# Moving four full-precision products of the last block ahead of its second layer, and weighing and adding half by half

## The reference, cut to what matters

```python
def expert_block(args):
    xblk, e = args
    return (jax.nn.silu(xblk @ w1[e]) * (xblk @ w3[e])) @ w2[e]

yb = lax.map(expert_block, (xb.reshape(n_blocks, MOE_BLOCK, D), block_e)).reshape(-1, D)
y = (yb[dest] * wts.reshape(-1)[order][:, None]).astype(xf.dtype)
return jnp.zeros_like(xf).at[tok].add(y)
...
x = x + gx2 * _moe(hx.reshape(-1, D), ...).reshape(x.shape)
return _rmsnorm(x, norm_f)
```

## Time and profile before

| | |
|---|---|
| median of 3 runs | 892.17 us (891.77 to 892.59) |
| the profiled execution's own time | 892.63 us |
| its span | 890.9 us |
| busy in the span: TensorE, VectorE, ScalarE, GpSimd | 858.4, 635.9, 415.1, 194.5 us |
| chain that ended last: TensorE, VectorE, DMA | 78%, 11%, 5% |

### The profile page before, as it was taken

How to read it: one execution, slowest core, us unless ns; L and a number is a source line. 1 busy time by engine, 2 the same in 40 slices (tenths; PEclk the granted TensorE clock), 3 DMA queues, 4 the chain that set the end, 5 groups by cost and what they waited for, 6 DMA issues and landing times.

```text
span 890.9 us, 14102 instructions
## 1 busy us (share of the span) xinstructions
PE 858.4 (96%) x4980; PEld 706.8 (79%) x4981; DVE 635.9 (71%) x907; ACT 415.1 (47%) x597; POOL 194.5 (22%) x225
## 2 busy tenths in 40 slices
PE   8999999999999999999879999999999999999993
PEld 6789878888997567887678888888888888888872
DVE  1678755789777748556875769399936648599995
ACT  3485456201224441232253457378634525487772
POOL 4042001100000101111033323233313222234324
PEclk9999999999999999999969999999999999999997
DMA  9953566511035032222799759979997596699984
GB/s 342 344 179 110 171 194 211 152 43 57 8 142 191 1 142 81 109 79 102 261 338 329 245 170 370 303 245 379 377 361 255 174 307 220 176 342 379 370 331 177
DMA packets 82359, 195.31 MB, mean 219 GB/s; under 512 B 4919, under 2 KB 13324, under 8 KB 82314
## 3 DMA queue, kind: packets, MB, share of 16 engines
q1 hardware_dynamic: 71168, 158.87, 49.6%
q0 software_dynamic: 8272, 25.84, 11.2%
q10 hardware_dynamic: 2874, 10.01, 2.8%
HBM read 169.57 MB, written 25.71 MB: 219 GB/s over the span
## 4 chain that ended last, share of the span: by engine, by line
PE 78%; DVE 11%; DMA 5%; issue 2%; ACT 2%; POOL 1%; ACTq 0%; SPq 0%; POOLq 0%; DVEq 0%
PE ps L2455 16%; PE ps L2443 12%; PE ps L2104 9%; PE ps L2460 8%; PE ps L2107 7%; PE ps L2437 2%; PE ps L2304 2%; DMA raw<-in_w_dram 2%; PE ps L2295 1%; DVE arena L1420 1%; PE ps L2297 1%; PE ps L2296 1%; DMA raw<-x_rows 1%; PE ps L2246 1%; PE ps L2160 1%
## 5 line engine op out<-in xcount | busy, mean ns | idle before, releaser
L1144 ACT ACTIVATE wah<-raw 128x2048 fp32r (+1 forms) x32 | 61.4, 1919 | 65.6 <-issue 32.8
L1853 DVE TENSOR_TENSOR wbl<-raw,wbh 128x2048 fp32r<-128x2048 f32 x32 | 73.1, 2288 | 5.2 <-ACT wbh L1144 4.5
L2443 PE MATMUL ps<-w2h,hTh 128*128 128x512 f32 x184 | 76.1, 413 | 0.5 <-DVE hTl L1863 0.5
L2455 PE MATMUL ps<-wbh,xTh 128*128 128x512 f32 x184 | 73.9, 402 | 0.0
L2455 PE MATMUL ps<-wah,xTh 128*128 128x512 f32 x184 | 72.3, 393 | 0.0
L775 POOL DMA_INDIRECT x_rows<-late_rows,block_dst x21 | 49.9, 2375 | 102.8 <-DVE late_rows L1868 102.8
L2443 PE MATMUL ps<-w2h,hTl 128*128 128x512 f32 x184 | 72.3, 393 | 0.0
L2443 PE MATMUL ps<-w2l,hTh 128*128 128x512 f32 x184 | 72.1, 392 | 0.0
L2455 PE MATMUL ps<-wal,xTh 128*128 128x512 f32 x184 | 72.1, 392 | 0.0
L1853 DVE TENSOR_TENSOR wal<-raw,wah 128x2048 fp32r<-128x2048 f32 x30 | 68.8, 2292 | 4.5 <-issue 3.2
L1853 DVE TENSOR_TENSOR w2l<-raw,w2h 128x2048 fp32r<-128x2048 f32 x32 | 71.8, 2282 | 0.0
(11 more groups left out here) (412 smaller groups left out, 2178.0 us busy)
## 6 DMA issues: line engine op xcount, KB each, us to landing
raw<-in_w_dram SPq DMA_DIRECT2D x64, 1024.0 KB
raw<-in_w_dram SPq DMA_DIRECT2D x16, 2048.0 KB
arena<-in_w_mod_dram SPq DMA_DIRECT2D x32, 512.0 KB, 4.1
arena<-in_x_dram SPq DMA_DIRECT2D x16, 512.0 KB, 9.7
arena<-in_w_mod_dram SPq DMA_DIRECT2D x3, 2048.0 KB, 13.7
arena<-in_w_in_dram SPq DMA_DIRECT2D x6, 1024.0 KB, 6.8
x_rows<-arena ACTq DMA_DIRECT2D x9, 512.0 KB, 3.1
hx_rows<-arena ACTq DMA_DIRECT2D x9, 512.0 KB, 4.4
```

The costliest lines, as they stand in the source:

```text
L1144: act.activation(high_half, raw_half, ACT.Copy).then_inc(w_high[j], 1)
L1853: dve.tensor_tensor(low_half, raw_half, high_half.bitcast(F32), ALU.subtract).then_inc(w_split[j], 1)
L2443: ins = pe.matmul(out_ap, parts[l][:, lhs], w_parts[w][:, cols], start=start and n == 0, stop=stop and n == 2)
L2455: pe.matmul(ps[:, 2 + j, :], xTh[:, k * P:(k + 1) * P], w[:, k * HALF:(k + 1) * HALF], start=(k == 0 and w is wh), stop=False)
```

## The change

The four full-precision products move from behind the last block's second layer to ahead of it, behind the first layer and ahead of the wait for the first half of `hTh` and `hTl`. They count on another semaphore (`rank_done` in place of `l2_done`), and they bring their waits with them. On VectorE the loop over weighing and the loop over adding become one, so that each half is weighed and then added; two increments of a counter go.

```diff
@@ VectorE, end of the last block
             for h in range(2):
                 dve.wait_ge(S["l2_done" if h else "l2_half"], last + 1)
                 weigh_half(last, h, last_y)
-            for h in range(2):
                 cols = slice(h * HALF, (h + 1) * HALF)
                 dve.wait_ge(S["y_ready"], 2 * last + (h + 3))
-                dve.wait_ge(S["l2_done"], last + (h + 2))
-                dve.sem_inc(S["load_seen"], 1)
+                dve.wait_ge(S["rank_done"], h + 5)
                 dve.tensor_tensor(last_x[:, cols], ps[:, h, :], last_y[:, cols], ALU.add).then_inc(S["last_sum"], 1)
@@ TensorE, expert(), after the first layer
                 if more:
                     turn_block(b + 1)
+                else:
+                    pe.wait_ge(S["slots_done"], 5)
+                    pe.wait_ge(S["gathered"], 16 * b + 48)
+                    pe.wait_ge(S["y_ready"], y_count)
+                    for h in range(2):
+                        cols = slice(h * HALF, (h + 1) * HALF)
+                        pe.matmul(ps[:, h, :], ident[:, :], last_x[:, cols], start=True, stop=False)
+                        pe.matmul(ps[:, h, :], same_tok, ysb[:, 0, cols], start=False, stop=True).then_inc(S["rank_done"], 1)
                 pe.wait_ge(S["hT_a"], b + 1)
                 pe.wait_ge(S["y_ready"], y_count)
@@ TensorE, after the last block
             expert(last, NE - 1, 2 * last + 2, False)
-            pe.wait_ge(S["slots_done"], 5)
-            pe.wait_ge(S["gathered"], 16 * last + 48)
-            for h in range(2):
-                cols = slice(h * HALF, (h + 1) * HALF)
-                pe.matmul(ps[:, h, :], ident[:, :], last_x[:, cols], start=True, stop=False)
-                pe.matmul(ps[:, h, :], same_tok, ysb[:, 0, cols], start=False, stop=True).then_inc(S["l2_done"], 1)
```

## The result

| | median | runs |
|---|---|---|
| before, 12 runs | 892.07 us | 890.80 to 892.59 |
| changed, 12 runs | 894.01 us | 892.38 to 894.26 |

The changed kernel is slower: the ratio is 1.0021, with a 95% interval of 1.0013 to 1.0028, that is 1.2 to 2.5 us. The forecast was 894.0.

A forecast was written before the change was run, and what follows sets the result against it. The last block was taken as bound by ScalarE, GpSimd's roots and VectorE, with TensorE's end products hidden. Terms 1.82 + 0.03 = 1.85 us on 892.17 gave 894.0 us; own range with run scatter 893.3 to 894.8, with rivals 892.3 to 895.4.

The forecast's parts named there:

- Steps 1 and 2: TensorE: products leaving the end (3.44 us) were hidden, worth nothing; at the new place they start at 865.92 without waiting.
- Step 3: TensorE behind the products: second layer starts 3.12 us later, shrinking to 2.11 us at the second hidden half's transposes.
- Step 4: ScalarE's copy of the second hidden half starts 0.42 us after the transposes, 1.82 us later than before.
- Step 5: Behind the copy: ScalarE's squares with GpSimd's roots, and VectorE's low part with its finishes, both move by 1.82 us.
- Step 6: VectorE weighing and adding half by half: 2.84 us in place of 2.60, net cost 0.03 us.
- step 7: Queue operations: two increments dropped on VectorE, nothing (-0.05 to 0); three more TensorE waits, nothing (0 to 0.1).
- Rival A: GpSimd's roots slip by one VectorE finish, 1.19 us more, about 895.2 us; chance 0.12 together with D.
- B: Rival: the delay on the way from ScalarE's copy to the weighing is absorbed, no change, 892.2 to 893.5; chance 0.15.
- C: Rival: VectorE's adds were waiting for TensorE's products, so moving them saves up to 1.5 us, 890.7; chance 0.07.
- D: Rival: a late gather holds the products at their new place, 1 us later giving 895.0; chance 0.12 together with Rival A.

The follow-up runs named there:

- e3: The changed kernel with the four products placed behind the transposes of the second hidden half: 891.91 us against 891.92 us for the kernel before.
- e5: The changed kernel with only half 0's two products ahead of the second layer, half 1's two left at the end: 892.21 us, ratio 1.0005 to the kernel before.
- e7: The changed kernel with ScalarE squaring row tile 7 ahead of its copy of the second hidden half: 893.11 us, ratio 1.0011 to the kernel before.
- e2: The kernel before with only VectorE's order changed to half by half, products left at the end: 892.38 us, ratio 1.0003.
- e1: The changed kernel with VectorE's old order (weigh, weigh, add, add), so only the products moved: 893.94 us against 891.92 us for the kernel before.
- e9: e2 with the end products counting on rank_done, so VectorE waits for constants and the counter increments are gone: ratio 1.0001 to the kernel before.
- e4: Against the kernel before: one product in TensorE's wait, half 0 weighed and added between finishes, early rows last, the two indirect stores swapped: ratio 0.9998.
- e8: Against the kernel before: tile 3's gain and ScalarE's second-half copy earlier, products behind six second-layer groups, half 0 behind tile 6, old store order: 890.47 us, ratio 0.9988.

## Why the prediction was right

It was right in direction, size and mechanism. That 894.0 met the median of 894.01 so closely is luck: its base was 0.10 us above the 892.07 of the twelve runs, and the cost by the medians, 1.94 us, was 0.09 above its sum of 1.85. The direction was given a chance of only 0.50. Step by step:

- Steps 1 and 2 (the products at the end are covered; the new place starts without a wait): right. They start 0.90 us behind the mark, forecast 0.92, and TensorE's end at mark + 10.2 is 3.2 us ahead of the first weighing. e3 shows the cover: the order of TensorE's work behind the transposes is free.
- Step 3 (transposes 2.11 us later): they came 1.99 later. The six second-layer products took 1.39 us (from 866.86 + 0.86 = 867.72 to 869.11) and not 1.49: the second of them came 0.23 us behind the first, where before, behind an idle TensorE, it came after 0.31. This is the only term that was off by more than 0.02 us.
- Step 4 (copy 1.82 us later, on ScalarE's reaction of 0.42 us): the reaction was 0.41, the delay 6.14 - 4.45 = 1.69. e5, with no delay at all for two products, shows that the idle places were counted rightly.
- Step 5 (both roads move alike, so GpSimd keeps its phase): the early rows' finish is released at the same distance, idle 0.43 us in both traces. e7 shows both roads.
- Step 6 (0.03 us for half by half): 2.85 us against 2.60, and the second store starts 6.80 us after the first weighing against 6.77. Right, but only because the wait and the increment of step 7 had left the queue: with them, in e2, the second store starts 7.20 us after the first weighing.
- Step 7 said that the dropped wait and increment are worth nothing. Where they stood that was so: in e1 they are gone and nothing is gained. In the new order they would have cost 0.19 us for each half (e2 against e9), so that part of the step was wrong, with no effect on the sum. The row that I read for it, 0.02 us, showed the instruction and not what it makes the next one wait.

The sum was 1.85 us; the traces give 1.72 and the medians 1.94. (The upper end of the range, by its own terms, is 892.17 + 2.3 + 0.42 = 894.9 and not 894.8.) Rival A (a slip of GpSimd by one finish) did not occur in any trace with the old order of finishes. B (absorbed) was wrong since VectorE's new idle time holds nothing that is late; e7 shows that it would hold the root of tile 7 if ScalarE squared first, and then 0.5 us are given back by the trace. C (the adds waited for TensorE) is refuted by e1 and e3: the end of TensorE's last product moved by -1.6 and -0.3 us, and the time by +2.0 and 0.0. D (a late gather): the products start 0.90 us behind the mark, with no wait, in the changed kernel and in e1, e5 and e7.

The Trainium skill (VectorE: DVE Perf Modes, The DRAIN you can't avoid) found, for eight copies in a row, that a semaphore between chained VectorE operations costs nothing extra. The prediction weighed this as a rule that would leave the four operations at 2.60 us; they took 2.85 in the changed kernel and in e9. For these operations the trace decides against it, by some 0.12 us for each add that stands right behind its weighing.

## What to carry to other kernels

Before moving work off an engine's tail, look whether the tail waits for it: here 3.4 us of TensorE work at the very end were hidden, and the same work 7 us earlier stood ahead of one short hand-over (two transposes) on which ScalarE, GpSimd and VectorE all hung. Count the idle places between the new position and the next hand-over, since here work up to their size (1.65 us) was free and everything beyond it was paid in full. And measure from a mark near the change: the ends of two single traces differed by 0.1 us where the change cost 1.7.

## What the runs showed of the hardware

A wait of VectorE against a register's value and an increment behind it, 0.06 us by their own rows, together held the next VectorE operation 0.19 us when they stood behind a wait that was met late (e2 against e9), and cost nothing when they ran while VectorE was busy (before against e1, 2.60 us for the four operations in both).

GpSimd's one-column power takes 0.54 to 0.56 us with VectorE idle. When it starts during a finish it takes 1.46 to 1.63 us and ends 0.39 to 0.42 us after that finish (875.45 against 875.05 before, 875.54 against 875.15 after; 870.29 against 869.88 before for the longest). It was not held by every VectorE operation: within an add that reads one input from the PSUM banks it took 0.54 us (872.76 in e4, 872.22 in e8), and where it had started 0.12 us ahead of a finish 0.55 (867.66 against 867.78 in e8).
